# MLP opening products computed inside the output projection's stage, and the third tile's attention rows queued ahead of the rest of x

## The reference

```
def _finish(x, oa, ob, w_o, g_mlp, w_up, w_down):
    o = jnp.concatenate([oa.reshape(bn, t, D_A), ob.reshape(bn, t, D_B)], axis=-1).astype(x.dtype)
    x = x + o @ w_o
    u = jax.nn.relu(_rmsnorm(x, g_mlp) @ w_up)
    return x + (u * u) @ w_down
```

## Time and profile before

| | before |
|---|---|
| median of 3 runs | 3765.91 us (3760.31 to 3769.47) |
| the profiled execution | 3767.08 us, span 3765.4 us |
| PE busy | 3523.0 us, 94% of the span |
| mean granted TensorE clock | 0.967 of full speed |
| `join_heads` of group 0 on PE | 1998.78 to 2122.5 us |
| `mlp` of group 0 begins on PE | 2130.57 us |
| `join_heads` of group 1 on PE | 2832.84 to 2972.4 us |
| `mlp` of group 1 begins on PE | 2978.26 us |

### The profile page before, as it was taken

One profiled execution on the slowest core, in us unless ns is written; L12 is line 12 of the kernel. 1 busy time (PEld: TensorE's weight loads), 2 busy tenths in 40 slices (PEclk: granted clock), 3 DMA queues, 4 the chain that ended last, 5 costly groups with the idle time before them and its releaser, 6 DMA issues. The chain is left out here.

```text
span 3765.4 us, 50230 instructions
## 1 busy us (share of the span) xinstructions
PE 3523.0 (94%) x18196; PEld 2746.5 (73%) x18240; DVE 1488.0 (40%) x2873; ACT 980.3 (26%) x1424; POOL 1102.6 (29%) x1030
## 2 busy tenths in 40 slices
PE   7999999699988899779997899999998899999999
PEld 7987788455546677644445788888886788888888
DVE  2223332565526565233322333443433333333333
ACT  3322322245541222222222311112113311111111
POOL 1224466477775555501331100000001100000000
PEclk9999999899999899889998999999999999999999
DMA  6546767866746765278874211111104111111111
GB/s 201 188 157 216 231 207 216 205 177 171 201 151 163 195 193 152 92 307 308 299 263 140 73 45 45 45 49 57 50 34 151 59 45 45 40 38 41 37 45 62
DMA packets 303528, 507.60 MB, mean 135 GB/s; under 512 B 48850, under 2 KB 190676, under 8 KB 297940
## 3 DMA queue, kind: packets, MB, share of 16 engines
q1 hardware_dynamic: 266356, 370.29, 32.7%
q10 hardware_dynamic: 23032, 80.04, 6.3%
q0 software_dynamic: 13952, 54.80, 4.0%
HBM read 408.18 MB, written 164.50 MB: 152 GB/s over the span
## 5 line engine op out<-in xcount | busy, mean ns | idle before, releaser
L2917 DVE TENSOR_TENSOR fin_x<-mlp_y,fin_x 128x512 f32<-128x512 f32 x544 | 350.4, 686 | 750.6 <-PE mlp_y L2960 750.6
L2877 POOL TENSOR_TENSOR mlp_u<-fox_in_squares 128x1024 f32<-128x1024 f32 (+2 forms) x80 | 131.6, 1645 | 1336.2 <-ACT fox_in_squares L2818 1336.2
L2937 PE MATMUL mlp_u<-fin_h_hi,fin_w_hi 128*128 128x512 f32 (+2 forms) x1280 | 451.6, 353 | 14.0 <-PEq L55 14.0
L2938 PE MATMUL mlp_u<-fin_h_lo,fin_w_hi 128*128 128x512 f32 (+2 forms) x1280 | 451.6, 353 | 0.0
L2939 PE MATMUL mlp_u<-fin_h_hi,fin_w_lo 128*128 128x512 f32 (+2 forms) x1280 | 451.3, 353 | 0.0
L2960 PE MATMUL mlp_y<-fin_w_hi,mlp_u_lo 128*128 128x512 f32 x1088 | 425.1, 391 | 0.0
L674 PE MATMUL proj_z<-proj_w_lo,proj_x_hi 128*128 128x512 f32 (+1 forms) x816 | 303.6, 372 | 0.0
L673 PE MATMUL proj_z<-proj_w_hi,proj_x_hi 128*128 128x512 f32 (+1 forms) x748 | 280.7, 375 | 10.7 <-DVE proj_w_lo L518 10.7
L675 PE MATMUL proj_z<-proj_w_hi,proj_x_lo 128*128 128x512 f32 (+1 forms) x748 | 275.6, 368 | 0.0
L2937 PEld LDWEIGHTS mlp_u<-fin_h_hi,fin_w_hi 128*128 128x128 f32 x1280 | 241.8, 189 | 37.5 <-issue 14.5
L2938 PEld LDWEIGHTS mlp_u<-fin_h_lo,fin_w_hi 128*128 128x128 f32 x1280 | 241.7, 189 | 22.2
(11 more groups left out here) (290 smaller groups left out, 6807.3 us busy)
## 6 DMA issues: line engine op xcount, KB each, us to landing
samp_v_in<-in_cache_v POOLq DMA_DIRECT2D x128, 256.0 KB, 4.8
fin_w_raw<-in_w_up SPq DMA_DIRECT2D x64, 512.0 KB, 3.8
fin_w_raw<-in_w_down SPq DMA_DIRECT2D x64, 512.0 KB, 4.0
out_new_win_k<-in_win_k ACTq DMA_DIRECT2D x8, 4080.0 KB
out_new_win_v<-in_win_v ACTq DMA_DIRECT2D x8, 4080.0 KB
samp_k_in<-in_cache_k SPq DMA_DIRECT2D x80, 256.0 KB, 4.8
proj_x_hi<-scratch_xt SPq DMA_DIRECT2D x34, 512.0 KB, 4.8
proj_x_lo<-scratch_xt SPq DMA_DIRECT2D x34, 512.0 KB, 5.8
```

The lines of the kernel that those rows point to most:

```text
L2917: dve.tensor_tensor(part, y_ps[(tiles * par + t) % 2][0:rows, q * D_G:(q + 1) * D_G], part, ALU.add).then_inc(y_added, 1)
L2937: pe.matmul(out, hi, h_hi[:, k, c0:c0 + n], start=(k == 0), stop=False)
L2938: pe.matmul(out, hi, h_lo[:, k, c0:c0 + n], start=False, stop=False)
```

## The change

Three things are changed, in both groups.

1. In `join_heads` SP queues the attention rows of the third tile (`load_o(2)`) between the first tile of x and the rest of x. They were behind the rest of x.
2. `up(0)`, the 48 products of the MLP's first block and first chunk, stands in `join_heads` in two halves of 24: `up_first(0)` between the two last turnings, `up_first(1)` after the last. The chunk is the first 4 tiles (3 in group 1). Its sums go into `u_first`, two PSUM banks that are now held over both stages: `join_heads` uses them as one of its two buffers for the projection, with the buffers' order swapped for an odd number of tiles so that the last tile is in the other one.
3. The split of the first two `w_up` pieces moves forward on ACT and DVE: it now stands at the head of the last tile's turn. ACT waits there for the first half of the last tile's products, since the pieces take the place of `w_o` columns that this half reads.

In `mlp` PE only counts `up_done` up by one where `up(0)` was; the wait for all four pieces (`w_split` at 4) before `body` of block 0 stays. The helper `token_chunks` is the computation of the chunks taken out of `mlp`.

```
-        pr_ps = [ph.ps(f"pr{j}", [P, D_MODEL]) for j in range(2)]
+        pr_ps = [u_first[:, :, :].rearrange("p f t -> p (f t)"), ph.ps("pr", [P, D_MODEL])]
+        if tiles % 2:
+            pr_ps.reverse()
...
             for n, (a, b) in enumerate(((0, 1), (1, tiles))):
                 sp.dma_start(x1[:, a:b, :], dram["x"][(first + a) * P:(first + b) * P, :]
                              .rearrange("(t p) n -> p t n", p=P)).then_inc(x_loaded[n], 16)
-            for t in range(2, tiles):
+                if n == 0:
+                    load_o(2)
+            for t in range(3, tiles):
                 load_o(t)
...
                 if t + 1 < tiles:
                     hi_o(t + 1)
+                else:
+                    act.wait_ge(product, 2 * tiles - 1)
+                    for q in range(2):
+                        act.wait_ge(w_in["loaded"][q], 16)
+                        act.activation(w_hi[:, q, :], w_in["raw"][:, q, :], ACT.Copy).then_inc(w_in["hi_done"], 1)
...
+            def up_first(f):
+
+                _t0, per, _c0, n = token_chunks(first, tiles)[0]
+                pe.wait_ge(w_in["split"], 2)
+                pe.wait_ge(h_lo_done, per)
+                pe.wait_ge(added, 2 * (tiles - 1))
+                out = pr_ps[tiles % 2][:, f * 512:f * 512 + n]
+                for k in range(KC):
+                    a = k % (KC // 2) * FBLK + f * P
+                    hi, lo = w_hi[:, k // (KC // 2), a:a + P], w_lo[:, k // (KC // 2), a:a + P]
+                    pe.matmul(out, hi, h_hi[:, k, 0:n], start=(k == 0), stop=False)
+                    pe.matmul(out, hi, h_lo[:, k, 0:n], start=False, stop=False)
+                    pe.matmul(out, lo, h_hi[:, k, 0:n], start=False, stop=(k == KC - 1))
...
                 if t > 0:
                     turn_h(t - 1)
+            up_first(0)
             turn_h(tiles - 1)
+            up_first(1)
...
-            pe.wait_ge(w_split, PIECES // 2)
-            up(0, 0, 0)
+            pe.sem_inc(up_done, 1)
             pe.wait_ge(w_split, PIECES)
```

More of the change, by code:

```diff
@@ L2502, in _, with token_chunks, join_heads @@
                     products(v, 1)
-def join_heads(nc, c, dram, g, first, tiles, h_hi, h_lo, x1, o_in, o_loaded, w_in, sent):
+def token_chunks(first, tiles):
+    tokens = min(tiles * P, (TILES - first) * P + N_SAMPLE)
+    per = -(-tiles // -(-tokens // 512))
+    return [(t, min(per, tiles - t), t * P, min(per * P, tokens - t * P)) for t in range(0, tiles, per)]
+def join_heads(nc, c, dram, g, first, tiles, h_hi, h_lo, x1, o_in, o_loaded, w_in, u_first, sent):
     with Phase(nc, f"join{g}") as ph:
@@ L2604, in _ @@
                     hi_h(t - 1)
[L2605 to L2608, removed]
             hi_h(tiles - 1)
@@ L2656, in _ @@
                     lo_o(t + 1)
+                else:
+                    for q in range(2):
+                        dve.wait_ge(w_in["hi_done"], q + 1)
+                        dve.tensor_tensor(w_lo[:, q, :], w_in["raw"][:, q, :], w_hi[:, q, :].bitcast(F32),
+                                          ALU.subtract).then_inc(w_in["split"], 1)
                 dve.wait_ge(product, 2 * (t + 1))
@@ L2674, in _ @@
                                   h_hi[:, :, t * P:t * P + n].bitcast(F32), ALU.subtract).then_inc(h_lo_done, 1)
[L2675 to L2679, removed]
         @block.tensor
@@ L2720, in _, with mlp @@
                     turn_h(t - 1)
+            up_first(0)
             turn_h(tiles - 1)
[L2724 to L2734, removed]
+            up_first(1)
+def mlp(nc, c, dram, g, first, tiles, h_hi, h_lo, x1, w_in, u_first, o_in, o_loaded, spare, out_sent):
+    chunks = token_chunks(first, tiles)
+    NCH = len(chunks)
     FB = FBLK // P
@@ L2748, in mlp @@
         u_lo = ph.sb("u_lo", [P, 2, FB, 512], F32R)
-        u_ps = [ph.ps(f"u{j}", [P, FB, 512]) for j in range(2)]
+        u_ps = [u_first, ph.ps("u_more", [P, FB, 512])]
         y_ps = [ph.ps(f"y{j}", [P, D_MODEL]) for j in range(2)]
@@ L3009, in finish @@
             h_lo = tile.sb("h_lo", [P, KC, tokens], F32R)
+            u_first = tile.ps("u_first", [P, FBLK // P, 512])
             x1 = tile.sb("x1", [P, tiles, D_MODEL])
@@ L3013, in finish @@
             w_in["lo"] = tile.sb("w_lo", [P, KC, D_MODEL], F32R)
-            join_heads(nc, c, dram, g, first, tiles, h_hi, h_lo, x1, o_in, o_loaded[g], w_in, sent)
-            mlp(nc, c, dram, g, first, tiles, h_hi, h_lo, x1, w_in, o_in, o_loaded[1], spare, sent)
+            join_heads(nc, c, dram, g, first, tiles, h_hi, h_lo, x1, o_in, o_loaded[g], w_in, u_first, sent)
+            mlp(nc, c, dram, g, first, tiles, h_hi, h_lo, x1, w_in, u_first, o_in, o_loaded[1], spare, sent)
 def build(nc, dram):
```

## The result

The changed kernel takes 3743.15 us (median of 4 runs, 3736.3 to 3749.06) against 3763.6 for the kernel before in the same comparison; the ratio is 0.994, with a 95% interval from 0.9919 to 0.9961, so about 23 us less, with 15 to 30 as its bounds. The profiled execution has a span of 3747.4 us.

A forecast was written before the change was run, and what follows sets the result against it. PE, busy 94% of the span, was taken as the bound, losing time only where it waits or runs slowly. Gains 7.7 + 8.5 + 3.8 + 2.1 = 22.1 us, against a median of 3765.91, gave 3744; range 3736 to 3755.

The forecast's parts named there:

- Part 1: Third tile in join_heads: attention rows moved forward end PE's wait and slow restart; 7.7 us in group 0, 8.5 in group 1.
- The rival by which they come no sooner: Third tile's attention rows: transfers in SP's queue share the engines, so the move gains nothing; 3760; chance 0.06.
- Part 2, group 0: Group 0's join end: idle 8.3 us before up(1), slow restart again, up(1) ends at 2151.5, not 2155.31; gain 3.8 us.
- Part 2, group 1: Group 1's join end: gain 1.3 us with slow up(1), plus 0.8 at the first down's wait; 2.1 in all.
- The step on DVE's splits: Group 0's join end: w_up splits take 3.6 us, ending at 2115.4, ahead of the last tile's adding at 2116.9.
- the ends: Rival at both join ends: the wait for pieces 2 and 3 eats all the gain there; 3750; chance 0.12.
- The clock: Rival at both join ends: clock falls during moved products, turning 5.9 us gain into 10.7 loss; 3760; chance 0.04.
- PE as the last at the barrier: Slower rival at the stage's end: everybody waits for PE, up to 19 us per group; 3782; chance 0.03.
- the better case: Rival at the MLP's start: the restart runs at full clock, 5.4 us more gained; 3738; chance 0.08.

The follow-up runs named there:

- products alone: The changed kernel with the third tile's attention rows put back behind the rest of x, only the moved products left; 3756.03 us, ratio 0.9985 to the kernel before.
- rows alone: The kernel before with only the third tile's attention rows started ahead of the rest of x, no products moved; 3749.89 us, ratio 0.9969.
- the last experiment: The changed kernel with one low part of h made by DVE ahead of its w_up splits instead of by GpSimd beside them; one run, 3737.5 us.
- wait later: The changed kernel with PE's wait for the four split pieces moved from ahead of up(1) to the first down product; 3748.74 us, ratio 0.9956 to before.
- kept warm: The changed kernel with 36 products of up(1) done an extra time while PE waits for pieces 2 and 3; 3743.98 us, ratio 0.9948 to before.

## Why the prediction was right

The forecast was 3744 and the median is 3743.15; the kernel before, at 3763.6 in the same comparison, was itself 2.3 below the 3765.91 that the forecast started from. The sum of 22.1 met 22.2 from the first turning on. The mechanisms were right in the main, but that the sum fits to 0.1 is luck, as its terms show.

Part 1, 7.7 and 8.5. From tile 1's last product of the first half to the turning of h PE took 6.38 and 6.34 us, forecast 6.2, so 7.5 and 8.36 were gained there. In group 1 the whole S1 gained only 6.6, chiefly for the slow stretch earlier in the stage (seven products, 1.4 us). It is not the change's: S1 in the seven further kernels with the first edit is 35.8 to 37.7. The rows landed 4.6 us before PE wanted them (2027.1, 2031.68), and the rest of x at 2036.1, ahead of the adding of tile 1, for which PE's products end at 2038.2. The rival by which they come no sooner is out. The Trainium skill, "DMA: Bandwidth & Descriptors", section "Queues, rings and completion order", says that on each DMA engine descriptors are taken in ring order, and does not promise that they complete in that order; the landings at 2025.9, 2027.1 and 2036.1, in the order of issue, agree.

Part 2, group 0, 3.8: measured 3.1. The barrier was 1.10, forecast 1.1, and `up(1)` took 13.69, forecast 13.86. What was too small is 7.20 for the pieces from SP's start to their split: 7.85 in this execution, though 7.07 to 7.24 in the five others in which DVE splits them first. The wait was 9.00 where I had 8.3.

Part 2, group 1, 1.3 and 0.8: measured 3.6 and 1.1, the term that was sized worst. I took 8.45 for the pieces and 10.70 for the slow `up(1)`, the one value each that the trace had; 6.99 and 9.92 came. The slow `up(1)` differs from execution to execution: 9.81 to 11.28 in the four kernels that have it, and with products alone, where it was 11.28, E1 gained 2.2. The pieces do not: 8.45 and, in rows alone, 8.94 belong to the kernels with `up(0)` in the MLP, and 6.99 to 7.31 stand in six kernels with moved products. So the term was taken from an arrangement that the change removes. The transfers themselves land sooner there (3.8 us after their start in the changed kernel's group 1, 5.3 before, as medians of the two); why, no run shows. These misses, +2.6 in group 1's end against -0.7 and -2.1 elsewhere, cancelled.

The step on DVE's splits was wrong in size and had no price by luck. I took 3.6 us from ACT's start to DVE's end, from a place where GpSimd stood idle; it was 4.8 (2113.08 - 2108.30), and of the 1.5 us between the splits and the last adding 0.43 were left. The Trainium skill, "SBUF — State Buffer", section "Who interferes with whom", says that a DVE instruction with two SBUF inputs contends with a GpSimd instruction that reads SBUF. The trace agrees, with 3.71 against 2.35, and the last experiment shows it by taking the GpSimd instruction away.

The rivals: the ends gave 6.8 when alone, not nothing. The clock was 1.00 through the moved products. PE as the last at the barrier cost 1.10, not up to 19, and its own first product came 1.34 us after the stage's end where it did not have to wait for pieces (wait later), so nothing of the size of that rival held it. The restart was at 1.2 GHz, so the better case did not come, and kept warm shows what it would have been worth: 3.4 us to the first `down` by the traces, of which 1.3 came back in group 1's M.

What the prediction did not see is behind its own place: had the wait ahead of `up(1)` been taken away at once, DVE's order in the first block would have asked for nearly all of it back.

## What to carry to other kernels

Moving work ahead of a wait pays for the part that stands inside another engine's latency: here moving 48 products gained 6 to 7 us with 24 of them inside PE's wait for the last normed tile, and nothing with all 48 behind it. That the other 24 earned nothing is argued, not shown. When a wait is removed, read the order of the engine that releases the next one, to the end of the first loop turn, since that is where the time comes back. And where executions differ by 20 us ahead of the change, compare distances from a mark common to both traces.

## What the runs showed of the hardware

Two DVE subtractions, each of two SBUF inputs, together took 3.71 us in place of 2.35 beside a GpSimd instruction that reads SBUF. When they began, at 2109.37, 1.50 us of that instruction were left, and the two took 1.36 longer; GpSimd's own 2.40 was what it was elsewhere in the stage (2.39 to 2.41).

The length of a wait alone did not settle PE's clock behind it. In the first tiles of a join PE waits for splits of `w_o`. Behind such a wait of 2.73 us, in wait later, the products are 0.43 apart at once:

```profile
2032.26 0.80 PE L2740 MATMUL fin_u_first<-fin_w_hi,join_o_hi 128*128 128x512 f32 x1 [2.73 <-DVE fin_w_lo L2664]
2032.85 0.63 PE L2741 MATMUL fin_u_first<-fin_w_lo,join_o_hi 128*128 128x512 f32 x1
```

Behind one of 2.67 us, in products alone, they are 0.23 apart, and stay so up to PE's next long wait:

```profile
2010.25 0.50 PE L2738 MATMUL fin_u_first<-fin_w_hi,join_o_hi 128*128 128x512 f32 x1 [2.67 <-DVE fin_w_lo L2662]
2010.59 0.39 PE L2739 MATMUL fin_u_first<-fin_w_lo,join_o_hi 128*128 128x512 f32 x1
```

Waits for these splits of 1.13, 1.40, 1.89, 1.94, 1.96, 2.19 and 2.35, in other executions, also had full clock behind them, while the 1.92 of the changed kernel had seven slow products; what decides is not shown. Waits of 7.84 to 9.00 ahead of `up(1)` had 1.2 GHz behind them every time. Where slow products followed, they cost between 1.4 us (seven of them, 0.43 apart instead of 0.23) and 3.0 (13.86 against 10.88 for 48 products).

A transfer of 512 KB queued behind another of 512 KB landed 1.2 us after it, with 3584 KB behind both. The large one landed 10.2 us behind the first (2036.1 and 2025.9), where it had landed 8.9 behind it in the kernel before (2031.1 and 2022.2), so the small one cost it about as much.
